# Router logits of a mixture-of-experts block: router weights stationary in four column groups, tokens moving, then one product with a 0/1 matrix

## The reference, cut to what matters

```python
def _hier_moe(h, wg, bg, we, be, w_exp_in, w_exp_out):
    t = h.reshape(-1, shape[-1])                       # 640 x 1024
    g_prob = jax.nn.softmax((t @ wg + bg), axis=-1)    # 4 groups
    g_p, g_idx = lax.top_k(g_prob, 1)
    e_logits = (t @ we + be).reshape(-1, N_GROUPS, EXPERTS_PER_GROUP)   # 16 experts
    e_prob = jax.nn.softmax(take_along_axis(e_logits, g_idx...), axis=-1)
    e_p, e_idx = lax.top_k(e_prob, TOP_K)
    ...
    hid = jnp.einsum("nd,edf->nef", t, w_exp_in)
```

## Time and profile before

| | us |
|---|---|
| median of three runs | 607.96 |
| lowest, highest | 605.49, 609.97 |
| span of the profiled execution | 602.5 |
| PE busy in the span | 535.8 (89%) |
| DVE busy | 363.1 (60%) |
| ACT busy | 273.6 (45%) |
| POOL busy | 90.8 (15%) |

### The profile page before, as it was taken

The page is one execution under the profiler, slowest core; times in us unless marked ns, Lnnn a source line. Parts: engine busy times, 40 slices in busy tenths (PEclk is TensorE's granted clock), DMA queues, the critical chain, the costliest instruction groups (busy, mean ns, idle before and its releaser), DMA issues.

```text
span 602.5 us, 8095 instructions
## 1 busy us (share of the span) xinstructions
PE 535.8 (89%) x3217; PEld 438.5 (73%) x3218; DVE 363.1 (60%) x583; ACT 273.6 (45%) x381; POOL 90.8 (15%) x122
## 2 busy tenths in 40 slices
PE   3798999999989998778999999879999999999660
PEld 0477888988769998556778888867788888887220
DVE  1236131443102040697856988875999999997885
ACT  1326130202113121676771212544888888885263
POOL 0005700001200000122100000021132122200531
PEclk9997999999999999998999999997999999999786
DMA  7997994474934312279409810658899999989677
GB/s 287 397 325 235 260 358 156 144 277 146 307 124 157 140 34 105 58 290 279 114 2 350 279 70 36 209 194 345 317 392 421 417 421 415 417 334 330 199 232 159
DMA packets 55263, 146.55 MB, mean 243 GB/s; under 512 B 7320, under 2 KB 16083, under 8 KB 49080
## 3 DMA queue, kind: packets, MB, share of 16 engines
q1 hardware_dynamic: 41800, 110.51, 50.6%
q0 software_dynamic: 10688, 33.90, 17.2%
q10 hardware_dynamic: 2736, 1.61, 0.9%
HBM read 127.60 MB, written 23.35 MB: 251 GB/s over the span
## 4 chain that ended last, share of the span: by engine, by line
PE 51%; DMA 17%; DVE 14%; issue 9%; ACT 5%; POOL 2%; SPq 1%; DVEq 0%; ACTq 0%; POOLq 0%
PE PS L1616 7%; PE PS L1618 7%; PE PS L1617 7%; PE PS L1671 6%; PE PS L1672 6%; PE PS L1676 6%; DMA raw<-in_w_ada 5%; DMA uni<-in_w_expert_out 5%; PE PS L1633 3%; DMA g<-in_x_prompt 3%; DVE act_lo L1369 2%; DMA uni<-bias_windows 2%; DVE w_lo L1301 2%; PE PS L1882 1%; PE PS L1869 1%
## 5 line engine op out<-in xcount | busy, mean ns | idle before, releaser
L1616 PE MATMUL PS<-w_hi,act_hi 128*128 128x512 f32 x252 | 102.0, 405 | 1.8 <-DVE act_lo L1390 0.9
L1671 PE MATMUL PS<-act_hi,w_hi 128*128 128x320 f32 x320 | 98.8, 317 | 1.7 <-ACT g L744 1.7
L1618 PE MATMUL PS<-w_hi,act_lo 128*128 128x512 f32 x252 | 98.6, 391 | 0.0
L1617 PE MATMUL PS<-w_lo,act_hi 128*128 128x512 f32 x252 | 98.5, 391 | 0.0
L1672 PE MATMUL PS<-act_lo,w_hi 128*128 128x320 f32 x320 | 97.0, 311 | 0.0
L1301 DVE TENSOR_TENSOR w_lo<-raw,w_hi 128x2048 fp32r<-128x2048 f32 x32 | 73.2, 2286 | 3.2 <-POOL small L626 2.0
L1676 PE MATMUL PS<-act_hi,w_lo 128*128 128x320 f32 x320 | 73.4, 311 | 0.0
L1671 PEld LDWEIGHTS PS<-act_hi,w_hi 128*128 128x128 f32 x320 | 60.9, 190 | 8.0 <-issue 3.4
L891 ACT ACTIVATE w_hi<-raw 128x2048 fp32r<-128x2048 f32 x32 | 61.2, 1913 | 9.7 <-DMA raw<-in_w_expert_in 6.1
L1672 PEld LDWEIGHTS PS<-act_lo,w_hi 128*128 128x128 f32 x320 | 60.8, 190 | 0.0
L1616 PEld LDWEIGHTS PS<-w_hi,act_hi 128*128 128x128 f32 x252 | 47.6, 189 | 13.3 <-issue 2.2
(11 more groups left out here) (244 smaller groups left out, 866.7 us busy)
## 6 DMA issues: line engine op xcount, KB each, us to landing
raw<-in_w_expert_in SPq DMA_DIRECT2D x32, 1024.0 KB, 11.7
raw<-in_w_ada SPq DMA_DIRECT2D x24, 1024.0 KB, 9.1
uni<-in_w_expert_out SPq DMA_DIRECT2D x16, 1024.0 KB, 11.0
raw<-in_w_in SPq DMA_DIRECT2D x12, 1024.0 KB, 9.7
expert_rows<-uni POOLq DMA_DIRECT2D x15, 512.0 KB, 8.0
expert_rows<-g POOLq DMA_DIRECT2D x2, 2560.0 KB, 12.2
g<-in_x_sample SPq DMA_DIRECT2D x2, 2048.0 KB, 13.9
raw<-in_w_out SPq DMA_DIRECT2D x4, 1024.0 KB, 8.2
```

Of the source, the lines that this page charges most:

```text
L1616: T.matmul(out, lh, rh, start=first, stop=False)
L1617: T.matmul(out, lh, rl, start=False, stop=False)
L1618: return T.matmul(out, ll, rh, start=False, stop=last)
L1671: T.matmul(out, a, h_hi[:, k, sl], start=f, stop=False)
```

## The change

The roles of the router product's operands are exchanged. `wr` is padded to 32 columns for each strip and zeroed whole; strip k's 32 columns are stationary in column group k % 4, so eight matmuls with 128 moving token columns leave four partial sums, transposed, on partitions 0 to 127 of bank 4. ACT copies them to SBUF (`logits_copy`), and one matmul, `router_fold`, with these 128x128 values stationary and a constant 128x24 matrix of zeros and ones moving, adds the four groups and turns the result to tokens on partitions, where the choice reads it as before. The fold stands ahead of (c, k) = (0, 7) of `mix_out`, nine matmuls behind the router; for tile 3 behind `gather_first(1)`, for tile 4 behind `rank(3)`. The router waits for both halves of `h2_T` at once. On ACT `logits_copy(n - 1)` stands behind `root(n)` for n = 1, 2, 3; for tile 3 it stands between `h2_copy(3)` and `root(4)`; for tile 4 behind `h2_copy(4)`. Two semaphores of the start-up are merged into `s_silu`, and `const` has 24 more columns.

```diff
-        wr = sb("wr", [P, KD, NR])
+        wr = sb("wr", [P, KD, 32])
+        group_fold = const[:, C_FOLD:C_FOLD + NR]
+        group_logits = uni[:, 7760:7760 + P]
...
-            nc.gpsimd.memset(wr[:, :, NG:E_AT], 0.0).then_inc(s_rpz, 1)
+            nc.gpsimd.memset(wr[:, :, :], 0.0).then_inc(s_rpz, 1)
...
+            def logits_copy(n):
+
+                act.wait_ge(s_lp, n + 1)
+                nc.scalar.activation(group_logits, PS[:, 4, 0:P], ACT.Copy).then_inc(s_lcp, 1)
...
             root(0)
-            for n in range(1, NT):
-                if n < NT - 1:
-                    normed(n - 1)
-                    h2_copy(n - 1)
-                    root(n)
+            for n in range(1, NT - 1):
+                normed(n - 1)
+                h2_copy(n - 1)
+                root(n)
+                logits_copy(n - 1)
...
             expert_whi(0, 0)
             h2_copy(NT - 2)
+            logits_copy(NT - 2)
             root(NT - 1)
             expert_whi(0, 1)
             h2_copy(NT - 1)
+            logits_copy(NT - 1)
...
                         if n >= 2 and (c, k) == (0, 4):
                             router(n - 2)
+                        if n >= 2 and (c, k) == (0, 7):
+                            router_fold(n - 2)
...
                 for k in range(KD):
-                    if k % 4 == 0:
-                        pe.wait_ge(s_h2c, 2 * n + 1 + k // 4)
-                    mm = T.matmul(PS[:, 2 if n == NT - 1 else 6, 0:NR], h2_T[:, k, :], wr[:, k, :], start=(k == 0), stop=(k == KD - 1))
-                mm.then_inc(s_lg, 1)
+                    if k == 0:
+                        pe.wait_ge(s_h2c, 2 * n + 2)
+                    g = k % 4
+                    mm = T.matmul(PS[32 * g:32 * g + 32, 4, 0:P], wr[:, k, :], h2_T[:, k, :], start=(k < 4), stop=(k >= 4))
+                mm.then_inc(s_lp, 1)
+
+            def router_fold(n):
+
+                pe.wait_ge(s_lcp, n + 1)
+                T.matmul(PS[:, 2 if n == NT - 1 else 6, 0:NR], group_logits, group_fold, start=True, stop=True).then_inc(s_lg, 1)
...
             router(NT - 2)
             gather_first(1)
+            router_fold(NT - 2)
             turn_h2(NT - 1)
             router(NT - 1)
             rank(NT - 2)
+            router_fold(NT - 1)
```

More of the change, by code:

```diff
@@ L68, in build @@
     C_SEL = C_COL + P
-    C_END = C_SEL + 2
+    C_FOLD = C_SEL + 2
+    C_END = C_FOLD + NR
     ctx = ExitStack()
@@ L235, in build @@
         s_small = sem("small_rows_loaded")
-        s_silu = sem("silu_steps")
+        s_silu = sem("silu_and_condition_steps")
         s_rows = sem("rows_transposed")
-        s_cols = sem("cols_ready")
         s_raw = [[sem(f"raw_{b}_half_{h}_loaded") for h in range(2)] for b in range(2)]
         s_ada = sem("ada_half_chunks_multiplied")
-        s_cond = sem("condition_ready")
         s_ar = sem("mod_sums_copied")
@@ L310, in build @@
         s_lg = sem("logits_sum_ready")
+        s_lp = sem("logits_by_group_ready")
+        s_lcp = sem("logits_by_group_copied")
         s_one = sem("choices_of_tile_ready")
@@ L1067, in _ @@
             dve.wait_ge(s_rows, 1)
-            V.tensor_copy(cols[:, :], PS[:, 0, 0:P]).then_inc(s_cols, 1)
-            dve.wait_ge(s_cols, 1)
-            V.tensor_copy(cond[:, :, 0:2], cols[:, 96:96 + 2 * KD].rearrange("p (j k) -> p k j", j=2)).then_inc(s_cond, 1)
+            V.tensor_copy(cols[:, :], PS[:, 0, 0:P]).then_inc(s_silu, 1)
+            dve.wait_ge(s_silu, 3)
+            V.tensor_copy(cond[:, :, 0:2], cols[:, 96:96 + 2 * KD].rearrange("p (j k) -> p k j", j=2)).then_inc(s_silu, 1)
             link(V.tensor_scalar(cols[:, 8:16], cols[:, 8:16], 1.0, None, ALU.add))
@@ L1678, in project @@
                     mm.then_inc(s_acc, 1)
-            pe.wait_ge(s_cond, 1)
+            pe.wait_ge(s_silu, 4)
             ada(0)
@@ L2063, in constants @@
                            np.tile(chunks, (P, 1)).astype(np.float32),
-                           np.eye(P, dtype=np.float32).reshape(P, 4, 32)[:, :, 0:2].sum(1)], axis=1).astype(np.float32)
+                           np.eye(P, dtype=np.float32).reshape(P, 4, 32)[:, :, 0:2].sum(1),
+                           np.eye(P, dtype=np.float32).reshape(P, 4, 32)[:, :, 0:24].sum(1)], axis=1).astype(np.float32)
 _INS = ["x_prompt", "x_sample", "cache_k", "cache_v", "c", "c_ctx", "w_ada", "b_ada", "w_in", "conv_w", "rpb", "w_out",
```

## The result

The changed kernel takes 609.6 us, the median of twelve runs (607.8 to 612.7), beside 606.1 us for the kernel before in the same comparison (twelve runs, 602.2 to 610.6). The ratio is 1.0061, with a 95% interval from 1.0033 to 1.0089: slower by 3.7 us, 2.0 to 5.4 (the two medians differ by 3.5; the ratio, estimated from the single runs, gives 3.7). The profiled execution spans 606.4 us, before 602.5. The forecast was slower by 3.2 us, with 611.2 as the time and 607.5 to 614.8 as the range. The difference is less than the 1% that the forecast held to be measurable: its size is known to no better than a factor of about two, and its cause has to be read from the traces.

What follows compares the result with a forecast made beforehand. PE bounds the projection loop and experts; between them a DVE, ACT and PE chain, DVE without slack from choice 2. Choice 2's 2.46 plus root 4's 0.73 make 3.2 us: 608.0 + 3.2 = 611.2 us, range 607.5 to 614.8.

Steps and rivals of the forecast that it cites:

- The router product: On PE, sixteen passes in four overlapping column groups: 0.75 us to the next matmul instead of 1.70; bounds 0.57 and 1.87.
- rival C: Router product on PE: the column groups do not overlap, time 614.6 us; chance 0.07.
- PE's gain per tile: Projection loop: shorter router less fold and slower next matmul, 1.70 - 0.75 - 0.23 - 0.10 = 0.62 us, if nothing waits.
- Latency of the logits: Router's start to DVE, through nine matmuls and the fold: 3.32 us instead of 1.90, 1.42 later for an unmoved router.
- Tile 0's wait: First fold waits for ACT's copy behind root 1: PE idles 2.5 us and is 1.66 us late at rank 0.
- Choices 1 and 2: Logits of tiles 1 and 2 reach DVE 3.08 and 2.46 us later; from choice 2 DVE has no slack.
- Root 4: ACT takes root 4 only after tile 3's copy; DVE gets it 3.19 us later, adding 0.73 us to the chain.
- Choice 4 and the first expert: Fold 4 stands behind rank 3: logits 3.2 to 3.4 us later; first expert 3.2 us later.
- rival B: Clock falls after the new gap at 340 to 342.4, perhaps again ahead of router 3: 612.8 to 614.2 us; chance 0.28.
- D: The clock fall at 407.6 does not recur, saving 3.0 us: not slower, 608.2 us; chance 0.13.
- E: The change gains PE's saving alone, 3 x 0.62 = 1.9 us: 606.1 us; chance 0.05.
- F: Part of the delay is absorbed among the experts, where a load may be waited for: about 609.5 us; chance 0.05.

Runs made afterwards that it cites:

- one group: Changed kernel with all eight router strips in one column group, partitions 0 to 31, copy and fold on 32 partitions; 614.6 us (eight runs), ratio 1.0119.
- both orders: Changed kernel with ACT's logits copies 0 to 2 ahead of roots 1 to 3 and root 4 ahead of logits copy 3; 605.6 us, ratio 1.0032.
- rank 0 later: Version with folds 3 and 4 first, with rank 0 ahead of (1, 6) instead of (1, 4) in the second projection; 604.0 us, ratio 0.9950.
- the version with the gap filled: Changed kernel with ten bf16 products of zeros on PE between gather_first(0) and router 3; 609.1 us, ratio 1.0065.
- the version with folds 3 and 4 first: Both orders and early fold, plus fold 3 ahead of gather_first(1) and fold 4 ahead of rank(3); 603.4 us, ratio 0.9972.
- the fold early: Both orders, plus the fold three matmuls behind the router instead of nine, ahead of (0, 5); 604.4 us, ratio 0.9995.
- the start-up edits: Kernel before with only wider wr, whole zeroing and 24 more const columns, without the merged semaphores; 607.5 us, ratio 1.0042.

## Why the prediction was right

**The router product, mis-sized by a little.** Forecast 0.75 us to the next matmul, measured 0.57. The 0.75 was 0.43 of streaming, 0.14 of entry and tail, and 0.17 of idle ahead of the product. The first two make exactly 0.57. The idle exists, but ahead of the product (the 0.17 had been read from a row of the weight loads, PEld, and not of PE): L1628 starts at 338.42 and the router 0.32 us later, where the usual distance is 0.227. So 0.57 + 0.10 are lost, not 0.75. No overlap (rival C) is refuted: with one group the same passes take 1.87 us, the upper bound in the forecast. The Trainium skill, TensorEngine Tiling (Array Packing), section Theoretical Speedup, gives up to 4x for a dimension of 32; measured are 1.87 / 0.57 = 3.3 between one group and four, which lies within it.

**PE's gain per tile.** Forecast 0.62 us. From router 1 to router 2 there are 14.48 us before (365.83 - 351.35) and 13.81 after (368.37 - 354.56): 0.67.

**Latency of the logits.** Forecast 3.32 us from the router's start to DVE, measured 357.68 - 354.56 = 3.12; before it was 1.90. Later by 1.22, not 1.42.

**Tile 0's wait.** Forecast: the fold waits for a copy behind root 1, PE idle 2.5 us, choice 0 later by 1.20. Measured: 2.24 and 1.06. The experiment with the copy ahead of the root showed the cause by removing it: the idle was gone and choice 0 back at 11.58. Router 1 came 1.55 us late (22.86 against 21.31), forecast 1.66.

**Choices 1 and 2.** Forecast +3.08 and +2.46, measured +2.77 and +2.10. The terms above give it: 1.55 + 1.22 = 2.77, and 1.55 - 0.67 + 1.22 = 2.10. So the 0.36 us by which the 2.46 was too high are 0.11 of tile 0, 0.05 of the gain and 0.20 of the latency.

**Root 4.** Forecast 0.73 us on the chain. Measured: `inverse(4)` later by 2.76 (53.96 against 51.20), choice 2 by 2.10, so 0.66; the experiment with root 4 ahead of the copy took 0.68 away by the order alone. In the second trace of the changed kernel, with router 3 at half clock, DVE's wait for the root was 1.02 us instead of 0.58: behind the copy, the root also takes over what the clock does to the router.

**Choice 4 and the first expert.** Forecast +3.2 to 3.4 and +3.2; measured +3.67 and +3.84. Up to choice 3 (+2.77) the sum was 0.4 too high, and then it was 0.6 too low: the clock was at 0.50 over 390.7 to 397.2, which the forecast had not put there. From choice 3 to choice 4 there are 3.33 us before, 3.61 in the second trace of the changed kernel, where the clock had come back for that stretch (1.00 over 392 to 396), and 4.23 in the first. So about 0.3 us are the change's (fold 4 behind `rank(3)`, as forecast) and 0.6 the clock's.

**The clock, rival B.** The fall that B placed at the new gap did not come: 1.00 over 340 to 384, with a gap of 2.24 us in it. B's second place, the 2.7 us gap ahead of router 3, did see falls. Six traces have a gap of 2.6 to 2.7 us there, and in four of them a fall starts inside it or within 1 us of router 3's start: the second trace of the changed kernel and the experiments with the copy ahead of the root, with one group and with both orders. Seven traces have a gap of 0.56 to 1.41 us there, and in none does a fall start so close; in two of these it comes 2.1 and 2.4 us behind router 3's start (rank 0 later, and the second trace of the kernel before, 0.74 over 385 to 398). So where the fall comes seems to follow the gap, as B had it. That there are more falls for it isn't seen: one somewhere between 382 and 401 is in 11 of the 13 traces, also in the two other traces with the old router and in the version with the gap filled (393 to 400). Only the first trace of before and the version with folds 3 and 4 first have none. It costs up to 1.7 us at the first expert and scatters both kernels.

The mean granted clock of the single runs tells the same: 0.963 for the changed kernel (12 runs) and 0.965 for the kernel before (78 runs in three comparisons), with a standard error of 0.0016 on the difference. Among the runs of the kernel before, 0.01 of clock goes with 2.5 to 4.1 us, so a part of some 0.4 to 0.6 us for the clock in the change's 3.7 is an estimate that can't be told from nothing.

**Rivals D, E and F.** In the first trace of the changed kernel the fall at 407.6 to 414.5 became one over 414.3 to 417.5, half as long, and of 3.84 us 2.2 remain at the end. But in the second trace of the kernel before it is as short, over 413.9 to 417.4:

```profile
413.90:417.40 3.50, 3.50 (x10) 2.73 (x9) 3.43 (x5) 1.94 (x2) 0.17 (x1) 0.53 0.93 323
```

So a fall half as long needs no change of the kernel, and neither D nor F is shown to have taken back anything by it; the ratio, slower by 3.7 us, shows nothing of either. E, the change's gain on its own, needed root, copy and folds in other places: the versions with the fold early and with folds 3 and 4 first. There the gain at the first expert was at most 1.2 us, not the 1.9 that three routers save, since from `rank(0)` on PE is ahead of DVE: a wait of 0.78 us, when moved, came back as 0.65 us at the next one.

So the change's own part, read with the clock at full speed, is 2.77 + 0.28 = 3.05 us against the forecast 3.2. The measured 3.7, with 2.0 to 5.4 as its interval, holds both; what the other 0.65 us are is not settled: the clock (0.4 to 0.6 us by the estimate above), the start-up edits (up to about 1 us not excluded) and chance are each enough. The mechanism was right, term by term. That 3.2 and 3.05 lie so close owes something to luck all the same: the terms of choice 2 and of root 4 made the sum 0.43 us too high (0.36 and 0.07), and the 0.28 of fold 4 between choices 3 and 4, which the sum left out, made up for most of it. The absolute time was off by another 1.9 us, since the kernel before had a median of 606.1 us over twelve runs and not 608.0.

## What to carry to other kernels

Making a small product three times shorter is worth nothing by itself when it adds a copy and a second product to the path of its consumer: count the latency from the first operand to the consumer, and give every new link the place in its queue where its data is ready, never behind an instruction that waits for later work. With those places put right (copies 0 to 2 ahead of their roots, root 4 ahead of copy 3, fold three matmuls behind instead of nine) the same idea went from 0.6% slower to no slower (0.9995), and with the last folds moved forward as well its first expert starts 1.21 us earlier than in the kernel before. The ratio, 0.9972, is then 0.3% below 1, a smaller step than the 0.4% that the start-up edits alone showed with an unchanged stage, so a gain in the whole time is likely and not sure. What a removed wait frees goes on only until the next wait for the same engine, so forecast from the engine that has no slack, here DVE from choice 2 on.

## What the runs showed that I had not expected

- ACT's copy out of PSUM takes the same time for 32 partitions (0.27 us) as for 128 (0.26 to 0.28).
- The granted clock falls to half in this stage in 11 of the 13 traces, both kernels among them, for 3.4 to 6.8 us at a time. Ten bf16 products in the largest gap did not keep it up in the one trace. The same `gather_first` of sixteen passes takes 2.03 to 2.05 us at full clock and up to 3.76 at half.
- Upstream, `root(0)` lies between 329.5 and 334.5 us over thirteen traces. Falls of the clock go with a late one: with none between 160 and 335 us it is at 329.5 (one trace), with some 3.4 us at half clock at 330.0 to 331.8, with some 10 us at 332.1 to 334.5; they don't explain all of it. Meanwhile the stage behind it of one kernel repeats within 0.02 us as long as the clock holds. To compare single traces, count from a mark ahead of the change and stop where the clock first differs.
